# A mixture-of-experts kernel: one chunk of the next expert's weights staged in spare SBUF, and the middle of each block reordered

## What is computed

```python
def moe(xt, w_router, b_router, w_up, b_up, w_down, b_down):
    gates = softmax over the top 4 of (xt @ w_router + b_router)
    for e in range(N_EXPERTS):
        hid = xt @ w_up[e] + b_up[e]
        x_glu = jnp.minimum(hid[:, :D_EXPERT], SWIGLU_LIMIT)
        x_lin = jnp.clip(hid[:, D_EXPERT:], -SWIGLU_LIMIT, SWIGLU_LIMIT)
        act = x_glu * jax.nn.sigmoid(SWIGLU_ALPHA * x_glu) * (x_lin + 1)
        y = act @ w_down[e] + b_down[e]
        out = out + gates[:, e:e + 1] * y
```

## Time and profile before

| | us |
|---|---|
| median of 3 runs | 1287.46 |
| lowest, highest | 1286.85, 1291.06 |
| the profiled execution's own time | 1288.93 |
| its span | 1287.2 |
| PE busy | 1207.2 (94%) |
| DVE busy | 372.5 (29%) |
| ACT busy | 185.8 (14%) |
| POOL busy | 59.2 (5%) |
| HBM read | 453.06 MB, mean 353 GB/s |
| chain that ended last | PE 52%, DMA 39%, DVE 4%, issue 2% |

### The profile page before, as it was taken

The page is one execution under the profiler, slowest core; times in us unless marked ns, Lnnn a source line. Parts: engine busy times, 40 slices in busy tenths (PEclk is TensorE's granted clock), DMA queues, the critical chain, the costliest instruction groups (busy, mean ns, idle before and its releaser), DMA issues.

```text
span 1287.2 us, 15187 instructions
## 1 busy us (share of the span) xinstructions
PE 1207.2 (94%) x5850; PEld 536.9 (42%) x5851; DVE 372.5 (29%) x737; ACT 185.8 (14%) x360; POOL 59.2 (5%) x89
## 2 busy tenths in 40 slices
PE   5899999889999999999999999999999999999996
PEld 1888655453343433333333333333443333333342
DVE  1944364631321112222111111122211122211114
ACT  2200264110111001110010000011110011101001
POOL 2230053000000000000000000000000000000000
PEclk9899999979999999999999999999999999999998
DMA  9973488309499999999999999999699999999590
GB/s 372 369 208 131 160 258 318 130 27 383 184 415 429 430 428 429 427 429 430 428 429 427 429 430 428 429 428 403 256 416 429 429 427 429 428 428 429 238 391 33
DMA packets 49044, 454.40 MB, mean 353 GB/s; under 512 B 16736, under 2 KB 16776, under 8 KB 20320
## 3 DMA queue, kind: packets, MB, share of 16 engines
q1 hardware_dynamic: 48064, 450.90, 84.7%
q0 software_dynamic: 512, 1.72, 0.4%
q10 hardware_dynamic: 448, 1.50, 0.4%
HBM read 453.06 MB, written 1.05 MB: 353 GB/s over the span
## 4 chain that ended last, share of the span: by engine, by line
PE 52%; DMA 39%; DVE 4%; issue 2%; ACT 1%; SPq 0%; POOL 0%; DVEq 0%; POOLq 0%
DMA ring<-in_moe_w_up 37%; PE pair L1201 23%; PE pair L1248 9%; PE pair L1010 9%; PE pair L1091 2%; DMA ring<-in_ada_w 2%; PE pair L1187 1%; PE pair L1026 1%; PE pair L968 1%; DVE hT_mem L899 1%; PE pair L1036 1%; PE pair L1049 1%; DVE v_mem L905 1%; DVE v_mem L906 1%; PE pair L1135 1%
## 5 line engine op out<-in xcount | busy, mean ns | idle before, releaser
L1201 PE MATMUL pair<-ring,v_mem 128*64 128x512 f32 x2240 | 495.8, 594 | 29.6 <-DMA ring<-in_moe_w_up 29.2
L1201 PEld LDWEIGHTS pair<-ring,v_mem 128*64 128x64 f32 x2240 | 181.1, 137 | 336.0 <-issue 274.5
L1248 PE MATMUL pair<-ring,v_mem 128*64 128x512 f32 x1120 | 248.1, 595 | 1.5
L905 DVE TENSOR_SCALAR v_mem<-pair 128x512 f32<-128x512 f32 x35 | 24.2, 692 | 719.8 <-PE pair L1211 719.8
L1248 PEld LDWEIGHTS pair<-ring,v_mem 128*64 128x64 f32 x1120 | 92.5, 137 | 132.9 <-issue 132.7
L579 ACT ACTIVATE v_mem<-v_mem 128x512 f32<-128x512 f32 x35 | 22.1, 630 | 538.8 <-DVE v_mem L905 538.8
L899 DVE TENSOR_TENSOR hT_mem<-hT_mem,pair 128x512 f32<-128x512 f32 x140 | 89.4, 680 | 8.0 <-PE pair L1187 8.0
L1187 PE MATMUL pair<-v_mem 64*128 64x512 f32 x280 | 78.8, 641 | 3.4 <-ACT v_mem L591 0.8
L1127 PE MATMUL pair<-q_mem,pT_mem 128*64 128x512 f32 x288 | 71.5, 618 | 1.3 <-DVE pT_mem L848 1.3
L379 POOL TENSOR_TENSOR rstd<-ms,neghalf 128x1 f32<-128x1 f32 (+1 forms) x8 | 4.7, 594 | 1071.7 <-DVE ms L627 1071.7
L591 ACT ACTIVATE v_mem<-pair 128x512 f32<-128x512 f32 x35 | 20.9, 597 | 228.7 <-PE pair L1248 228.7
(11 more groups left out here) (217 smaller groups left out, 944.5 us busy)
## 6 DMA issues: line engine op xcount, KB each, us to landing
ring<-in_moe_w_up SPq DMA_DIRECT2D x128, 2048.0 KB, 23.2
ring<-in_moe_w_down SPq DMA_DIRECT2D x64, 2048.0 KB, 20.3
ring<-in_ada_w SPq DMA_DIRECT2D x24, 1024.0 KB, 8.4
ring<-in_na_w_qkv SPq DMA_DIRECT2D x12, 1024.0 KB, 27.4
ring<-in_na_w_o SPq DMA_DIRECT2D x4, 1024.0 KB, 15.1
tokens<-in_na_rpb SPq DMA_DIRECT2D x32, 96.0 KB, 6.4
gain<-in_norm_g POOLq DMA_DIRECT2D x3, 512.0 KB, 5.7
tokens<-in_x SPq DMA_DIRECT2D x1, 1024.0 KB, 5.0
```

The costliest lines, as they stand in the source:

```text
L905: d.tensor_scalar(glu, bank[0][:, :], LIMIT, None, ALU.min).then_inc(glu_ready, 1)
L1201: last = mm(bank[half][64 * n:64 * n + 64, :], xT[:, k % 4, 64 * (k // 4):64 * (k // 4) + 64], w[:, c0:c0 + HALF], start=k == 0, stop=False)
L1248: last = mm(bank[2][64 * n:64 * n + 64, :], aT[:, j, 64 * half:64 * half + 64], w[:, HALF * n:HALF * n + HALF], start=k == 0, stop=k == KC ...
```

## The change

- Three attention buffers (`kT_mem`, the token and bias buffer, `v_mem`) become one tensor `zone`; chunk 0 of an expert is no longer loaded into its home in the ring, but into `zone[:, 0:2]` (where the keys were), as soon as the chunk 0 before it has been copied out. POOL copies it home in 8 pieces of 512 columns when `ring_free` allows, and raises `staged[0]`, on which PE now waits in place of `expert_in[0]`. Chunk 0 of expert 0 is still loaded straight into the ring, and chunk 0 of expert 1 is loaded before chunks 4 and 5 of expert 0.
- "Gated half first": the last chunk of "up" is done for bank 0 with its bias, then for bank 1. DVE's clamp and its product with the sigmoid come before `up_done`, the product with the linear half last.
- "One-pass sums": `comb` is 0 or 1, without the gate; two small matmuls bring the gate to the slots, y is scaled by it and split into `y_high` and `y_low` (both of fp32r type, as `combT` now is), and a combine is four fp32r matmuls in place of two fp32 ones. The very first block's sums (line 1179) stay as they are.
- Buffers move to make room: the block's work tiles from `v_mem` to `hT_mem` and the modulation tiles, x1 to the buffer of the adaLN rows, b_up to the place of the probabilities. So b_up and x are loaded later (after the last attention matmul and after the last broadcast), the split of the up bias comes after gate2 on DVE, ACT's squares wait for that split, and ACT issues the DMA of b_down between the squares of the second token tile.

```diff
-            def expert(e, blocks_before):
-                for j in range(PER):
-
-                    sp.wait_ge(ring_free, blocks_before * PER + (EXP - PER + j + 1))
-                    load_expert(e, j)
-
-            for j in range(PER):
-                sp.wait_ge(ring_free, EXP - RING + 2 * j + 2)
-                load_expert(0, j)
+            for j in range(4):
+                sp.wait_ge(ring_free, EXP - RING + 2 * j + 2)
+                load_expert(0, j, expert_chunk(j))
+            sp.wait_ge(s_done, DUOS)
+            sp.wait_ge(expert_in[0], 16)
+            load_expert(1, 0, staged_chunk(0))
+            for j in range(4, PER):
+                sp.wait_ge(ring_free, EXP - RING + 2 * j + 2)
+                load_expert(0, j, expert_chunk(j))
+
+            def second_half(e):
+
+                blocks_before = sp.value_load(ends_i[0:1, bass.ds(e - 1, 1)], min_val=1, max_val=E + MAX_EXTRA)
+                for j in range(STAGED, PER):
                     sp.wait_ge(ring_free, blocks_before * PER + (EXP - PER + j + 1))
-                    load_expert(e, j)
-
+                    load_expert(e, j, expert_chunk(j))
+
             sp.wait_ge(tables_ready, 1)
-            with sp.Fori(1, E) as e:
-                blocks_before = sp.value_load(ends_i[0:1, bass.ds(e - 1, 1)], min_val=1, max_val=E + MAX_EXTRA)
-                expert(e, blocks_before)
+            with sp.Fori(1, E - 1) as e:
+                second_half(e)
+                for j in range(STAGED):
+                    sp.wait_ge(staged[j], e + 1)
+                    load_expert(e + 1, j, staged_chunk(j))
+            second_half(E - 1)
...
+            with pool.Fori(1, E) as e:
+                blocks_before = pool.value_load(ends_i[0:1, bass.ds(e - 1, 1)], min_val=1, max_val=E + MAX_EXTRA)
+                for j in range(STAGED):
+                    pool.wait_ge(expert_in[j], e * 16 + 16)
+                    pool.wait_ge(staged[j], e)
+                    pool.wait_ge(home_free[j], e)
+                    pool.wait_ge(ring_free, blocks_before * PER + (EXP - PER + j + 1))
+                    mark = staged_mark[:, j:j + 1]
+                    g.tensor_tensor(home_mark[:, j:j + 1], mark, mark, ALU.add).then_inc(home_free[j], 1)
+                    for i in range(8):
+                        c = slice(HALF * i, HALF * i + HALF)
+                        last = g.tensor_copy(expert_chunk(j)[:, c], staged_chunk(j)[:, c])
+                    last.then_inc(staged[j], 1)
...
-            sc.wait_ge(s_done, DUOS)
+            sc.wait_ge(o_done, DUOS)
+            sc.dma_start(bup, b_up[0]).then_inc(in_bup, 16)
+            sc.wait_ge(bc_done, 8)
             sc.dma_start(x1, token_rows(x)).then_inc(in_res, 16)
-            sc.wait_ge(bias_used, DUOS)
-            sc.dma_start(bup, b_up[0]).then_inc(in_bup, 16)
-            sc.dma_start(bdown, b_down[0]).then_inc(in_bdown, 16)
+            sc.wait_ge(bup_split, 1)
...
                 sc.wait_ge(x1_ready, t + 1)
+                if t == 1:
+                    sc.dma_start(bdown, b_down[0]).then_inc(in_bdown, 16)
...
+                s.activation(gate_slot, bank[4][:, TOK:TOK + 1], ACT.Copy).then_inc(slot_gates, 1)
                 s.activation(combT, bank[4][:, 0:TOK].rearrange("p (t s) -> p t s", t=2), ACT.Copy).then_inc(combT_ready, 1)
...
-                s.activation(y, bank[2][:, :], ACT.Copy).then_inc(y_ready, 1)
+                sc.wait_ge(slot_gates, b + 1)
+                s.activation(y_high, bank[2][:, :], ACT.Copy, scale=gate_slot).then_inc(y_ready, 1)
...
+                ve.wait_ge(y_ready, b + 1)
+                d.scalar_tensor_tensor(y_low, bank[2][:, :], gate_slot, y_high, ALU.mult, ALU.subtract).then_inc(y_split, 1)
...
                 for n in range(2):
-                    mm(bank[banks[n]][:, :], combT[64 * n:64 * n + 64, t, :], y[64 * n:64 * n + 64, :],
-                       start=True, stop=True).then_inc(part_done, 1)
+                    mm(bank[banks[n]][:, :], combT[64 * n:64 * n + 64, t, :], y_high[64 * n:64 * n + 64, :],
+                       start=True, stop=False)
+                for n in range(2):
+                    mm(bank[banks[n]][:, :], combT[64 * n:64 * n + 64, t, :], y_low[64 * n:64 * n + 64, :],
+                       start=False, stop=True).then_inc(part_done, 1)
...
-                for k in range(KC):
+                for k in range(KC - 2):
...
+                expert_chunk_here(pe, e, UPS - 1)
                 pe.wait_ge(bsel_ready, b + 1)
...
+                up(0, KC - 2)
+                up(0, KC - 1)
+                add_bias(0).then_inc(glu_done, 1)
+                up(1, KC - 2)
+                up(1, KC - 1).then_inc(ring_free, 1)
+                add_bias(1).then_inc(up_done, 1)
```

More of the change, by code:

```diff
@@ L42 @@
 ADA0, QK, VV, ADA1, ADA2, WO, EXP = 0, 8, 16, 20, 28, 36, 40
-PER, UPS = 6, 4
+PER, UPS, STAGED = 6, 4, 1
+ZONE = 6
 BIAS_SLOTS, BIAS_ROWS = 10, 6
@@ L188, in build @@
         wo_done, x1_ready, h2_ready = sem("wo_done"), sem("x1_ready"), sem("h2_ready")
+        staged = [sem(f"staged{j}") for j in range(STAGED)]
+        home_free = [sem(f"home_free{j}") for j in range(STAGED)]
         h2T_done, h2T_ready, logit_done = sem("h2T_done"), sem("h2T_ready"), sem("logit_done")
@@ L776, in _ @@
                 d.scalar_tensor_tensor(scale2[:, h], bank[i][:, :], 1.0, gain[:, h], ALU.add, ALU.mult).then_inc(bc_dve, 1)
+            ve.wait_ge(in_gain, 48)
+            for i in range(2):
+                ve.wait_ge(bc_done, 6 + i + 1)
+                h = slice(HALF * i, HALF * i + HALF)
+                d.tensor_tensor(gate2[:, h], bank[2 + i][:, :], gain[:, h], ALU.mult).then_inc(bc_dve, 1)
+            ve.wait_ge(bc_dve, 6)
             ve.wait_ge(in_bup, 16)
@@ L784, in _ @@
             d.tensor_copy(bup_parts[2 * E:3 * E, :], bup).then_inc(bup_split, 1)
-            ve.wait_ge(in_gain, 48)
-            for i in range(2):
-                ve.wait_ge(bc_done, 6 + i + 1)
-                h = slice(HALF * i, HALF * i + HALF)
-                d.tensor_tensor(gate2[:, h], bank[2 + i][:, :], gain[:, h], ALU.mult).then_inc(bc_dve, 1)
             ve.wait_ge(in_res, 16)
@@ L1206, in block_step @@
                         make_tables()
+                expert_chunk_here(pe, e, UPS - 1)
                 pe.wait_ge(bsel_ready, b + 1)
-                for half in range(2):
-                    for n in range(2):
-                        c0 = D * half + HALF * n
-                        last = mm(bank[half][64 * n:64 * n + 64, :], bsel, bup_parts[:, c0:c0 + HALF],
-                                  start=False, stop=True)
-                last.then_inc(up_done, 1)
+                up(0, KC - 2)
[4 more added lines that the diff above has]
+                add_bias(1).then_inc(up_done, 1)
                 if is_first:
@@ L1222, in block_step @@
                 for t in range(2):
-                    last = tr(bank[4][:, P * t:P * t + P], comb[:, t, :, :].rearrange("p a s -> p (a s)"), ident[:, :])
+                    tr(bank[4][:, P * t:P * t + P], comb[:, t, :, :].rearrange("p a s -> p (a s)"), ident[:, :])
+                for t in range(2):
+                    last = mm(bank[4][:, TOK:TOK + 1], comb[:, t, :, :].rearrange("p a s -> p (a s)"), gate_tok[:, t:t + 1],
+                              start=t == 0, stop=t == 1)
                 last.then_inc(combT_done, 1)
```

131 lines of the change are left out of this document (79 added, 52 removed).

## The result

The changed kernel takes **1368.5 us** (median of 4 runs, 1366.03 to 1374.28) against 1287.15 (4 runs, 1286.57 to 1291.06): a ratio of 1.0632, 95% interval 1.0607 to 1.0657. The forecast was 1285.8, within 1280 to 1292. The profiled execution took 1369.37 us, its span is 1367.6 and its mean granted clock 0.940 (0.985 before).

A forecast was written before the change was run, and what follows sets the result against it. DMA of 384 MB, its idle at the start and three two-block experts, and PE's final work were taken as the bound. +0.45 + 2.0 - 4.25 + 0.1 = -1.7 us from the median 1287.46 gave 1285.8, range 1280 to 1292.

The forecast's parts named there:

- the copy home: Before chunk 0 of each expert: POOL's copy takes 5.4 us, PE lags 1.0 us, paid at two two-block experts, +2.0 us.
- the estimate of 0.44: POOL copy: time in us per piece by the Trainium skill's one-input rate; copy 3.9 us, no lag, sum 2 us lower.
- the rival of the slow copy: POOL copies at its two-input price, 1.53 us a piece; PE lags 8.2 us, twice: 1300.2 us; chance 0.11.
- the clock of the restart: After a two-block expert: chunk 4's release, not chunk 0's, sets when loads go on, 20.4 us after the old restart.
- What bounds the kernel before: Expert part: DMA time of 384 MB, plus DMA idle at start and three two-block experts, plus PE's work after the last weights.
- The staged chunk is worth nothing: At restarts: 2 MB more lands in 11.5 us of idle time, but chunk 4 still waits until 20.4 us; gain nothing.
- Copy, 0.62 us a piece, +2.0 us: POOL's eight pieces plus 0.4 us for mark and semaphores; PE 1.0 us late, paid at the second and third two-block experts.
- The middle: From `up_done` to "down": 5.4 us in place of 6.1, gain 0.65 a middle, seven count, less 0.3: 4.25 us gained.
- the fp32r pairs: In combine: the two matmuls of a pair overlap, 0.5 us in place of 1.1; rival without overlap 1290.4 us, chance 0.12.
- Between attention and experts: Before the first expert block: b_down's DMA issue on ACT delays the path, +0.45 us, bounds 0 and 3.
- The tail from the last "down" on: Kernel end: y needs a second step (`y_low`), while the first sum gets 0.6 shorter; +0.1 us.
- The middles of all other blocks are hidden: Expert blocks: only seven middles count toward the time; a shorter middle elsewhere gains nothing.

The follow-up runs named there:

- the PSUM operand: Changed kernel, but DVE's two clamps write back to PSUM, so each product reads one tensor from PSUM; staging and all copies stay: 1285.07 us, ratio 0.9985.
- no staging: Changed kernel without the staged chunk and POOL's copies, chunk 0 loaded straight to its ring home: 1284.18 us, ratio 0.9981.
- half copy: Changed kernel with only four of the eight pieces copied, the rest of chunk 0's home keeping old weights: 1283.66 us, ratio 0.9971.
- copy in "down": Changed kernel, but POOL starts a copy only after DVE's copy of the transposed activation, just ahead of "down": 1286.36 us, ratio 0.9989.
- six pieces: Changed kernel with six of the eight pieces copied, a quarter of the copy left out: 1310.52 us, ratio 1.0178.

## Why the prediction was wrong

**The step that failed is the copy home.** It was costed as one thing, PE's wait for the last piece: "8 x 0.62 + 0.4 = 5.4", lag 1.0 us, +2.0 in all. The size was good (0.56 us a piece from start to start, 4.49 for eight, between the estimate of 0.44 and the 0.62 that was taken; PE waited 0.88 us where nothing collided). What was left out is what the copies do to DVE: the forecast took the two engines as working side by side. The text had the sentence "DVE works beside it", but as a remark inside the rival of the slow copy, at no price. The price is 3.77 us on DVE in a middle, of which PE waits 3.36, and 1.6 us of lower clock behind it: 4.94 us a block, 27 times. The rule on shared ports that the Trainium skill states would have been the rival that ended on the slow side; it was not weighed.

**A second step hid the first.** The copy was placed only in the DMA-bound stretch: chunk 0 lands at 612.5, behind the middle (601.9 to 608). In that stretch the forecast is right, as the copies at 611.9 with the PSUM operand show. But after each two-block expert PE is behind, and there chunk 4's release sets both the next copy and the next middle, 17.6 and 17.4 us later. The text had worked out that release as "the clock of the restart" and followed it to the loads, not to the copy behind them. A cost of 4.9 us a block in a stretch that was catching up by 2.1 (now 2.65) us a block turns the stretch into the rest of the kernel.

Point by point:
- **What bounds the kernel before:** right. Without collisions (no staging, half copy, copy in "down") the slices are back at about 425 to 431 GB/s.
- **The staged chunk is worth nothing:** right. At the second restart w_down is issued at 929.35 without staging and 929.71 with it (half copy), and the times don't differ.
- **Copy, 0.62 us a piece, +2.0 us:** right where it meets nothing (+0.9 with the PSUM operand, +2.2 in "down", both against no staging and neither clear of the intervals). Where it meets the product the same copies cost 83 us more.
- **The middle:** 5.4 us forecast, 329.39 - 323.82 = 5.57 measured, 6.1 before. A gain of 0.55 against 0.65; the fp32r pairs do overlap. The sum without staging was -4.25 + 0.45 + 0.1 = -3.7, measured -3.0 (-1.4 to -3.6 by the interval).
- **Between attention and experts:** the first expert block starts at 277.09, before 276.94: +0.15 against +0.45. The tail from the last "down" on is 14.7 us against 14.3: +0.4 against +0.1.
- **"The middles of all other blocks are hidden":** true only as long as PE's block stays under 29.4 us. Blocks with six pieces (30.5) and with four (27.9) stand on either side of that line.

## What to carry to other kernels

Work on POOL does not simply run beside DVE's: before placing a run of POOL operations, list the DVE operations that may fall into it, and give each that has all its tensors in SBUF up to the length of the whole run (all three kinds seen here stood). An operand in PSUM, or another place in the block, took nearly all of the cost away here. Where a transfer's release and the compute it disturbs hang on the same event, work out the phase in each regime, the catching-up one too, and compare the disturbed block with the round that hides it: below it a stall costs nothing, above it every block pays.

## What the runs showed of the hardware that was not expected

- Beside POOL's copies these DVE operations stood until the last copy's end: the two-input fp32 product (0.69 to 4.46 us), the one-input bf16 cast, 96x64 (0.18 to 3.82), and two TENSOR_SCALAR of 128x128 in fp32 (0.48 to 4.05 for both). Those with a PSUM operand did not: the additions (1.28 us for two), the product in PSUM form (0.69).
- Eight copies back to back keep DVE out for all eight. A single one over 4096 columns takes 3.59 us, eight over 512 take 4.49.
- It works the other way too: a 1x1 POOL operation that began 0.06 us behind a DVE product took 0.68 us instead of 0.18.
- Behind 3.4 us without a matmul the granted clock went from 1.00 to 0.50, and "down" took 7.8 us instead of 7.09. Unused matmuls in the gap made the kernel 11 us faster.
- Not settled: why DVE doesn't get in between two pieces. No kernel put a gap between them, so whether that would help is open.
